# Two transformer layers on one core: the product of weights and values as fp32r over two turned query blocks, issued ahead of the dense units

## The reference

```
def dilated_attention(q, k, v):          # three windows, merged here into one table of biases
    s = q @ k.T * HEAD_DIM ** -0.5 - slope * distance, masked;  p = exp(s - max)
    o = (p @ v) / sum(p)
y_b = dilated_attention(q, k, v) * silu(b_gate)
...
def stick_breaking_mixer(h, k, v, ...):
    z = einsum('bhtd,bhsd->bhts', q, k)                       # per block of 128 queries
    suffix = cumsum(log_keep, axis=3, reverse=True) - log_keep
    weights = where(strict, exp(log_sigmoid(z) + suffix), 0.0)
    o = einsum('bhts,bhsd->bhtd', weights, v)
    return (o * silu(gate)) @ w_out
```

## Time and profile before

| | |
|---|---|
| median of 3 runs | 3656.97 us (3647.4 to 3661.76) |
| profiled execution | 3654.47 us, its span 3652.8 us |
| TensorE busy | 3334.1 us |
| mean granted clock of TensorE | 0.942 of full |
| attention loop, first seven pairs / last | 566 to 1131 us / to 1183 us |
| stick-breaking loop, first seven pairs / last | 2696 to 3346 us / to 3421 us |

### The profile page before, as it was taken

How to read it: one execution, slowest core, us unless ns; L and a number is a source line. 1 busy time by engine, 2 the same in 40 slices (tenths; PEclk the granted TensorE clock), 3 DMA queues, 4 the chain that set the end, 5 groups by cost and what they waited for, 6 DMA issues and landing times. The chain is left out here.

```text
span 3652.8 us, 45164 instructions
## 1 busy us (share of the span) xinstructions
PE 3334.1 (91%) x16644; PEld 2762.9 (76%) x16644; DVE 1664.7 (46%) x2233; ACT 1315.7 (36%) x1783; POOL 539.9 (15%) x430
## 2 busy tenths in 40 slices
PE   6999989999998999698988889888889999998899
PEld 5788878888887777475866767666678888887777
DVE  4343224444444332556556565565434455454333
ACT  4332114444444222323222331223245555555331
POOL 3110000000000001212020020210223333332110
PEclk9999999999999999699999999999889999998799
DMA  2111222211211222012121121211211111111221
GB/s 89 44 52 54 69 69 61 67 60 53 64 52 58 99 78 77 20 48 57 47 58 42 46 64 42 52 47 58 76 35 41 41 41 41 41 41 47 98 69 58
DMA packets 85626, 206.06 MB, mean 56 GB/s; under 512 B 6816, under 2 KB 42272, under 8 KB 85184
## 3 DMA queue, kind: packets, MB, share of 16 engines
q1 hardware_dynamic: 74048, 164.66, 14.6%
q0 software_dynamic: 11392, 38.80, 3.7%
HBM read 165.56 MB, written 21.10 MB: 51 GB/s over the span
## 5 line engine op out<-in xcount | busy, mean ns | idle before, releaser
L119 DVE TENSOR_TENSOR wlo<-wraw,whi 128x1024 fp32r<-128x1024 f32 x208 | 282.0, 1356 | 388.0 <-ACT whi L114 384.7
L114 ACT ACTIVATE whi<-wraw 128x1024 fp32r<-128x1024 f32 x208 | 218.7, 1052 | 525.4 <-PE ssm_pT L127 155.0
L2117 DVE TENSOR_TENSOR_SCAN stick_keep<-stick_keep 128x128 f32<-128x128 f32 (+7 forms) x128 | 188.4, 1472 | 198.4 <-ACT stick_rows L2038 198.2
L125 PE MATMUL ssm_D<-x1hi,whi 128*128 128x512 f32 x640 | 262.1, 410 | 4.5 <-DVEq L1691 4.4
L125 PE MATMUL b_D<-x1hi,whi 128*128 128x512 f32 x640 | 255.3, 399 | 9.9 <-DVE att_k_low L950 8.5
L127 PE MATMUL ssm_D<-x1hi,wlo 128*128 128x512 f32 x640 | 254.5, 398 | 0.0
L126 PE MATMUL ssm_D<-x1lo,whi 128*128 128x512 f32 x640 | 254.3, 397 | 0.0
L127 PE MATMUL b_D<-x1hi,wlo 128*128 128x512 f32 x640 | 251.6, 393 | 0.0
L126 PE MATMUL b_D<-x1lo,whi 128*128 128x512 f32 x640 | 251.4, 393 | 0.0
L125 PE MATMUL stick_D<-x1hi,whi 128*128 128x512 f32 x512 | 221.2, 432 | 6.5 <-DVE x1lo L152 6.5
L2258 POOL TENSOR_TENSOR stick_rows<-stick_rows,stick_keep 128x128 f32<-128x128 f32 (+7 forms) x128 | 161.6, 1263 | 342.4 <-DVE stick_keep L2117 342.4
(11 more groups left out here) (376 smaller groups left out, 7528.8 us busy)
## 6 DMA issues: line engine op xcount, KB each, us to landing
wraw<-w_dram SPq DMA_DIRECT2D x208, 512.0 KB, 3.6
sq<-acum_rows SPq DMA_DIRECT2D x32, 512.0 KB, 9.0
att_bias<-alibi_dram SPq DMA_DIRECT2D x16, 512.0 KB, 3.6
stack<-stack POOLq DMA_DIRECT2D x32, 256.0 KB, 3.3
x_sb<-xT_dram SPq DMA_DIRECT2D x8, 512.0 KB, 8.2
branch_a<-sq POOLq DMA_DIRECT2D x8, 512.0 KB, 3.5
stack<-att_q_low POOLq DMA_DIRECT2D x16, 256.0 KB, 3.5
y_b<-att_y POOLq DMA_DIRECT2D x8, 512.0 KB, 3.0
```

The source lines that it names most:

```text
L114: act.activation(self.whi[:, s, :, :], self.wraw[:, s, :, :], ACT.Copy).then_inc(self.w_hi, 1)
L119: dve.tensor_tensor(self.wlo[:, s, :, :], self.wraw[:, s, :, :], self.whi[:, s, :, :].bitcast(F32), ALU.subtract).then_inc(self.w_lo, 1)
L125: pe.matmul(out, self.whi[:, s, w0, :], xhi[:, k, cols], start=start, stop=False)
L2117: dve.tensor_tensor_scan(k, k, k, 1.0, ALU.mult, ALU.bypass).then_inc(scan, 1)
```

## The change

The product of weights and values is turned round. The values are stationary, as a high and a low part in fp32r, side by side in 128 columns (`v0` for head 0: high, low; `v1` for head 1: low, high), so that the high part's result lies on one half of pO's partitions and the low part's on the other. What moves are the turned weights of two query blocks at a time (a unit u: rows 2u and 2u+1), 256 columns, as high part (`w_high`, a ScalarE copy) and low part (`w_low`, a VectorE subtraction). A group is two key blocks of a unit (up to 512 columns, 384 where the last block belongs to the second row alone). A unit of u % 4 = 0, 1, 2, 3 has 1, 2, 3, 4 groups, 20 in a pair; `turns_of` gives the slots in which they are turned: 2u+2 and 2u+3. Slot 3 and slot 11 get none; slots 2, 4, 5, 7, 10, 12, 13, 15 one; slots 6, 8, 9, 14, 16, 17 two.

In a slot TensorE now takes: scores of row `slot`; `values` of the groups that were turned in slot-1; the dense units; `turn_weights` of this slot's groups. The result needs no turning back. ScalarE takes one half of pO to `part` (`part_y`), VectorE adds the other (`add_y`), in the odd slots from 5 on, and at the pair's end multiplies by the gate once. In attention the rows are normalised on VectorE before they are turned (up to 1024 columns each). `rows` becomes a ring of four rows. v is split when it has been turned (`high_v`, `low_v`), now in slots 17 and 18. The low part of q is written by VectorE straight to the other half of the partitions, with no transfer; attention computes k, q, v, gate in this order (the weights' order in memory follows). The zeroing of k_low moves from VectorE to GpSimd. The stick stage is changed in the same way, without a normalisation; its `low_weights`, `add_y`, `part_y`, `high_v`, `low_v` are the same and lie at the `v_turn` steps 12 and 13.

`norm_diag` goes in all ten norms: `norm_spread` now transposes rtok's columns, each broadcast to 128 columns, in eight transposes.

The diff, cut to its core (attention stage; lines left out as "..."):

```diff
-    def norm_diag(self, dve, diag_done):
-
-        diag = self.sq[:, 0, :].rearrange("p (c t) -> p c t", c=NC)
-        dve.tensor_tensor(diag, self.ident[:, :].unsqueeze(1).to_broadcast([P, NC, P]),
-                          self.rtok[:, :].unsqueeze(2).to_broadcast([P, NC, P]), ALU.mult).then_inc(diag_done, 1)
-
-    def norm_spread(self, pe, spread, diag_done, spread_done):
-        pe.wait_ge(diag_done, 1)
-        for half in range(2):
-            last = pe.matmul(spread[:, half * H:half * H + H], self.ones[:, :],
-                             self.sq[:, 0, half * H:half * H + H], start=True, stop=True)
+    def norm_spread(self, pe, spread, rtok_done, count, spread_done):
+
+        pe.wait_ge(rtok_done, count)
+        for c in range(NC):
+            last = pe.transpose(spread[:, c * P:c * P + P], self.rtok[:, c:c + 1].to_broadcast([P, P]),
+                                self.ident[:, :])
...
-T_GROUPS = [(i + 4) // 4 for _, i in ROWS]
-T_BEFORE = [sum(T_GROUPS[:r]) for r in range(17)]
-T_PAIR = T_BEFORE[16]
+U_GROUPS = [u % 4 + 1 for u in range(8)]
+U_BEFORE = [sum(U_GROUPS[:u]) for u in range(9)]
+G_PAIR = U_BEFORE[8]
+ROW_AT = [(0, 640, 1408, 2304)[r % 4] for r in range(16)]
+ROW_COLS = 3328
+
+
+def turns_of(slot):
+
+    return [(u, g) for u in range(8) for g in range(U_GROUPS[u])
+            if slot == 2 * u + 2 + int(g >= (U_GROUPS[u] + 1) // 2)]
 
...
-    TV, TQ, TK, TG = range(4)
+    TK, TQ, TV, TG = range(4)
...
-        vN, gT, y_sb = (sb(n, [P, 2, S]) for n in ("vN", "gT", "y"))
+        gT, y_sb = sb("gT", [P, 2, S]), sb("y", [P, S])
+        v0 = ctx.enter_context(nc.sbuf_tensor("att_v0", [P, NC, P], F32R))
+        v1 = ctx.enter_context(nc.sbuf_tensor("att_v1", [P, 2, NC, P], F32R))
+        w_high = ctx.enter_context(nc.sbuf_tensor("att_w_high", [P, 2, H], F32R))
+        w_low = ctx.enter_context(nc.sbuf_tensor("att_w_low", [P, 2, H], F32R))
+        part = sb("part", [P, 2 * P])
...
-                        pe.wait_ge(stacked, 64 * p + 64)
+                        pe.wait_ge(q_lo, p + 1)
+                        pe.wait_ge(stacked, 32 * p + 32)
...
-                def turn_weights(p, r):
-                    h, i = ROWS[r]
-                    pe.wait_ge(ex, 16 * p + (r + 1))
-                    for g in range(T_GROUPS[r]):
-                        n = T_BEFORE[r] + g
-                        pe.wait_ge(tcopy, T_PAIR * p + (n + 1))
-                        for b in range(4 * g, min(4 * g + 4, i + 1)):
-                            last = pe.transpose(turned[n % 2][:, (b % 4) * P:(b % 4) * P + P],
-                                                rows[:, r % 2, b * P:b * P + P], K.ident[:, :])
-                        last.then_inc(turn, 1)
-                def values(p, q, r):
-                    h, i = ROWS[r]
-                    if r == 0:
-                        pe.wait_ge(v_copy, 2 * p + 3)
-                    pe.wait_ge(tcopy, T_PAIR * p + (T_BEFORE[r + 1] + 2))
-                    pe.wait_ge(yn, 16 * p + (r + 1))
-                    for b in range(i + 1):
-                        last = pe.matmul(pO[:, 0:HD], wT[:, r % 2, b * P:b * P + P],
-                                         vN[:, q, b * P + HD * h:b * P + HD * h + HD],
-                                         start=b == 0, stop=b == i)
+                def turn_weights(p, u, g):
+                    j, n = u % 4, U_BEFORE[u] + g
+                    pe.wait_ge(even, 16 * p + (2 * u + 2))
+                    pe.wait_ge(t_lo, G_PAIR * p + (n + 1))
+                    col = 0
+                    for b in (2 * g, 2 * g + 1):
+                        for r in (2 * u, 2 * u + 1):
+                            if b <= ROWS[r][1]:
+                                at = ROW_AT[r] + b * P
+                                last = pe.transpose(turned[n % 2][:, col:col + P], rows[:, at:at + P], K.ident[:, :])
+                                col += P
+                    last.then_inc(turn, 1)
+                def values(p, q, u, g):
+                    h, j, n = u // 4, u % 4, U_BEFORE[u] + g
+                    if u == 0:
+                        pe.wait_ge(v_lo, 2 * p + 2)
+                    pe.wait_ge(t_lo, G_PAIR * p + (n + 3))
+                    if g == 0:
+                        pe.wait_ge(y_add, 8 * p + (u + 1))
+                    for b in (2 * g, 2 * g + 1):
+                        v = v1[:, q, b, :] if h else v0[:, b, :]
+                        lone = b == 2 * j + 1
+                        c0 = P if lone else 0
+                        at = 2 * P * (b - 2 * g)
+                        pe.matmul(pO[:, c0:2 * P], v, w_high[:, n % 2, at:at + 2 * P - c0], start=b == 0, stop=False)
+                        last = pe.matmul(pO[:, c0:2 * P], v, w_low[:, n % 2, at:at + 2 * P - c0],
+                                         start=False, stop=lone)
                     last.then_inc(pv, 1)
-                def turn_y(p, g):
-                    if g == 0:
-                        pe.wait_ge(yn, 16 * p + 17)
-                    pe.wait_ge(tcopy, T_PAIR * p + (T_PAIR + 2))
-                    for c in range(4):
-                        last = pe.transpose(turned[g][:, c * P:c * P + P], yN[:, 4 * g + c, :], K.ident[:, :])
-                    last.then_inc(y_turn, 1)
 
                 def pair(p, q, more):
                     u = 0
@@ -748,27 +752,22 @@
                         if slot < 16:
                             score(p, q, slot)
                         n_units = UNITS[slot] if more else int(slot < 2 * KT)
+                        for unit, g in turns_of(slot - 1):
+                            values(p, q, unit, g)
                         units(p + 1, u, u + n_units)
                         u += n_units
-                        if 1 <= slot <= 16:
-                            if slot == 1:
-                                pe.wait_ge(y_out, 2 * p + 2)
-                            turn_weights(p, slot - 1)
-                        if 2 <= slot <= 17:
-                            values(p, q, slot - 2)
-                        if more and slot in (8, 9):
-                            turn_v(p + 1, slot - 8)
-                    for g in range(2):
-                        turn_y(p, g)
+                        for unit, g in turns_of(slot):
+                            turn_weights(p, unit, g)
+                        if more and slot in (17, 18):
+                            turn_v(p + 1, slot - 17)
 
...
+                def high_v(p, q, g):
                     act.wait_ge(v_turn, 2 * p + (g + 1))
                     if not (isinstance(p, int) and p == 0):
-                        act.wait_ge(pv, 16 * p - 14)
-                    act.activation(vN[:, q, g * H:g * H + H], pV[:, :], ACT.Copy).then_inc(v_copy, 1)
+                        act.wait_ge(pv, G_PAIR * p + (U_BEFORE[4] + 2 - G_PAIR))
+                    v = pV[:, :].rearrange("p (c d) -> p c d", d=P)
+                    act.activation(v0[:, 4 * g:4 * g + 4, 0:HD], v[:, :, 0:HD], ACT.Copy)
...
-                def copy_weights(p, r):
-                    h, i = ROWS[r]
-                    act.wait_ge(pv, 16 * p + (r + 1))
-                    for g in range(T_GROUPS[r]):
-                        n = T_BEFORE[r] + g
-                        act.wait_ge(turn, T_PAIR * p + (n + 5))
-                        cols = (min(4 * g + 4, i + 1) - 4 * g) * P
-                        act.activation(wT[:, r % 2, g * H:g * H + cols], turned[n % 2][:, 0:cols],
-                                       ACT.Copy).then_inc(tcopy, 1)
+                def high_weights(p, u, g):
+                    n = U_BEFORE[u] + g
+                    cols = 3 * P if g == u % 4 else 4 * P
+                    act.wait_ge(turn, G_PAIR * p + (n + 5))
+                    act.wait_ge(pv, G_PAIR * p + (n + 1))
+                    act.activation(w_high[:, n % 2, 0:cols], turned[n % 2][:, 0:cols], ACT.Copy).then_inc(t_hi, 1)
+                def part_y(p, u):
+                    h = u // 4
+                    act.wait_ge(pv, G_PAIR * p + (U_BEFORE[u + 1] + 2))
+                    act.wait_ge(y_add, 8 * p + (u + 1))
+                    act.activation(part[HD * h:HD * h + HD, :], pO[HD - HD * h:P - HD * h, 0:2 * P],
+                                   ACT.Copy).then_inc(y_part, 1)
 
                 def pair(p, q, more):
                     for slot in range(19):
                         if slot == 0 and not more:
                             split(p + 1, 1)
+                        for unit, g in turns_of(slot - 1):
+                            high_weights(p, unit, g)
+                        if slot in range(5, 19, 2):
+                            part_y(p, slot // 2 - 2)
                         if slot < 16:
                             weights(p, slot)
                         if slot == 1:
                             gate(p, q)
-                        if 1 <= slot <= 16:
-                            copy_weights(p, slot - 1)
                         if more:
...
```

(59 more changed lines are left out.)

368 lines of the change are left out of this document (188 added, 180 removed).

## The result

| | before | after |
|---|---|---|
| median, us | 3655.05 (3647.4 to 3661.76, 4 runs) | 3954.77 (3952.32 to 3961.89, 4 runs) |
| span of the profiled execution, us | 3652.8 | 3960.4 |
| ratio | 1 | 1.0817, 95% interval 1.0801 to 1.0832 |

What follows compares the result with a forecast made beforehand. TensorE's queue was the bound. Attention +120, stick +136, eighth pairs +12 and +10, norms -12, start -3: +263 on 3654.5 us gives 3917, taken as 3905; range 3790 to 4020.

Steps and rivals of the forecast that it cites:

- The chosen mechanism: In both loops, TensorE waits after the scores for copy and subtraction, plus work queued ahead on ScalarE and VectorE; 60%, 3850 to 3975.
- Rival (a): Both loops: ScalarE's and VectorE's queues are absorbed by longer slots, leaving the short chain only; +165, 3820 us; chance 20%.
- the short chain: Per slot, ScalarE's copy and VectorE's subtraction, less the scores' time: 18.7 us of waits per attention pair, 17.7 in stick.
- (c): Both loops: high and low parts are ready when the scores end, wait per slot under 0.49 us; faster, 3530 with none; 4%.
- (d): Both loops: no change to speak of, waits of 0.5 us per slot; 3650 us; chance 2%.
- Rival (b): TensorE's clock falls in the loops, 7 to 18 us per pair on top; 4000 to 4150 us; chance 14%.
- TensorE's own work: Each pair: 15.1 us of value matmuls become 9.6, yN's transposes and pair-end waits give 1.4; a gain of 6.9 us.
- the waits of both loops: TensorE's idle time before value matmuls, per pair with dense work: 18.7 + 5.4 us in attention, 17.7 + 8.7 in stick.
- the eighth pairs: Last pair of each loop: attention 63 us against 52 from a row's chain on VectorE, +12; stick taken as +10.
- the gain outside the loops: Ten norms -12 us; at the start of attention, first scores need one transfer less, -3 us.
- late queues: ScalarE and VectorE work queued ahead of high or low parts: 5.4 us per attention pair, 8.7 in stick.
- The norms: Ten norms: norm_diag leaves, 1.225 us each; norm_spread's four matmuls become eight transposes of about the same time; -12 us.

## Why the prediction was right, and where its terms were not

It said 3905 us, and 3954.8 was measured, within the range. The chosen mechanism holds: TensorE waits for VectorE's low part between scores and first value product, and the order does it. Rival (a), the short chain alone (3820), is out by 135 us; rivals (c) and (d) are out. Rival (b) is there in its mild form, on top of the forecast instead of in its place. That the sum came out no further off is in part luck: of the +263 us forecast and the +307.6 measured on the profiled executions, TensorE's own work was put 108 us too low, the waits of both loops 45 us and the eighth pairs 11 us too high, and the gain outside the loops 8 us too small. These errors run against each other.

By the windows, per pair with dense work, in us:

| | attention, predicted | measured | stick, predicted | measured |
|---|---|---|---|---|
| TensorE busy | -6.9 | +3.0 | -6.9 | -1.3 |
| TensorE idle | +18.7 + 5.4 = +24.1 | +22.7 | +17.7 + 8.7 = +26.4 | +21.3 |
| pair | +17.2 | +25.7 | +19.5 | +20.0 |

(Measured: busy 576.72 / 7 against 555.64 / 7 and 628.54 / 7 against 637.68 / 7; idle is the rest of each window. The -6.9 held 0.5 us of waits at the pair's end.)

**The waits** were right in attention (24.1 predicted, 22.7 measured) and 5 us too long in stick-breaking, where the 8.7 us of late queues were the weak estimate. In attention they can be compared slot by slot, idle time in front of the value products in us, mean of seven pairs:

| slot | 3 | 5 | 6 | 7 | 8 | 9 | 10 | 11 | 13 | 14 | 15 | 16 | 17 | 18 |
|---|---|---|---|---|---|---|---|---|---|---|---|---|---|---|
| predicted, with late queues | 0.9 | 1.5 | 0.6 | 3.85 | 1.65 | 2.1 | 0.9 | 1.5 | 3.6 | 0.6 | 1.45 | 1.85 | 2.4 | 1.3 |
| measured | 2.6 | 1.5 | 0.4 | 3.2 | 1.0 | 2.0 | 0.7 | 1.5 | 2.9 | 0.3 | 1.4 | 1.2 | 2.35 | 0.65 |

The short chain is right nearly everywhere, the late queues of slots 7, 8, 13 and 16 are each priced 0.6 to 0.7 us too high (for slot 7 the prediction's own figures, 5.55 less 3.4, give 2.15 us and not 2.4), and one late queue was overlooked, that of slot 3. ScalarE computes the gate in slot 1, and its two table loads stand ahead of the exponential of slot 2 and so of slot 3's high part:
```profile
1107.79 1.28 ACT L796 ACT_TABLE_LOAD   x1
1109.09 1.06 ACT L796 ACTIVATE att_gT<-att_gT 128x1024 f32<-128x1024 f32 x1
1110.16 1.28 ACT L812 ACT_TABLE_LOAD   x1
...
1112.07 0.47 ACT L821 ACTIVATE att_w_high<-att_turned 128x384 fp32r<-128x384 f32 x1
```
Scores of this slot were done by 1110.7, the products began at 1113.3. The prediction had counted such loads in stick-breaking only.

**TensorE's own work** is the step that was mis-sized. It was to fall by 6.9 us a pair, and rose by 3.0 in attention and fell by 1.3 in stick-breaking. Two things the runs tell apart.

Where few waits are left (values behind the units, k and q moved, 5.6 us idle a pair, clock 1.00) attention's own work is 522.7 / 7 = 74.7 us, 4.7 less than the 79.4 of before. From one start to the next, without the idle time, the value products took 15.0 us a pair before and take 10.1 there, 0.127 each where I had 0.12. The first product of a slot costs 0.22 us where it had to wait for its low part, and 0.11 where it had not; in that run:
```profile
908.43 0.28 PE L744 MATMUL att_pO<-att_w_high,att_v 128*128 128x256 f32 x1
908.55 0.28 PE L745 MATMUL att_pO<-att_w_low,att_v 128*128 128x256 f32 x1
```
The transposes of yN give 0.8 us. The remaining difference is mostly no work: the dense matmuls just ahead of the products grew by 1.3 us a pair, as the first 0.16 us of a wait lie under the end of the matmul before it and count as busy.

The other 7.7 us of attention come with the waits: 82.4 us a pair at a clock of 0.93. Dense matmuls at 0.42 us behind a wait, as shown above, are the 1.2 GHz level of the clock against 0.23 us at 2.4 GHz. A mean clock of 0.93 over 745 us means some 15 us a pair at the lower level, and if TensorE works in all of it, 15 x (1 - 0.23 / 0.425) = 7 us of it are lost, an estimate. In stick-breaking the same working gives some 4 us more than before (0.92 over 790 us against 0.95 over 650). I had set this case aside since attention's eighth pair kept full clock with idle time in it; with waits in every slot that no longer held, and after the change the eighth pair itself has 0.89. A chance of 14% was too little for it, and as an addition of some 7 us a pair it belonged in the sum. The Trainium skill (TensorE: Matmul & The Clock Gate, The HAM clock gate) says that idle lowers the clock; attention's traces agree, 0.93 with 24 us idle a pair, 0.97 with 7.4, 1.00 with 5.6. Idle time is not all of it: in stick-breaking the clock was 0.95 before, with 1.8 us idle a pair, and no run shows why.

**The eighth pairs**: +12 and +10 predicted; 62 us for 52 is +10, 76 for 75 is +1. Stick's last pair was already set by its chain of scan, GpSimd and copies, which the change leaves.

**The norms**: -12 predicted, -21 measured alone. The step that failed is "four matmuls become eight transposes of about the same time in all". At full clock, in the first norm of before and of after:
```profile
50.53 1.88 PE L216 MATMUL v_turned<-sq,ones 128*128 128x512 f32 x4
```
```profile
49.76 1.04 PE L211 MATMUL v_turned<-ident,rtok 128*128 128x128 f32 x8
```
And in a norm of the dt stage, at half clock:
```profile
1515.27 3.78 PE L216 MATMUL dt_spread<-sq,ones 128*128 128x512 f32 x4
```
```profile
1710.72 1.97 PE L211 MATMUL dt_spread<-ident,rtok 128*128 128x128 f32 x8
```
So each norm saves 0.8 to 1.8 us here, on top of the 1.2 us of the diagonal matrix.

**normalise**: the forms of the operation after (busy us, mean ns):
```profile
L925 DVE TENSOR_SCALAR att_rows<-att_rows,att_rinv 128x1024 f32<-128x1024 f32 x16 | 12.1, 753 | 0.6
...
L925 DVE TENSOR_SCALAR att_rows<-att_rows,att_rinv 128x512 f32<-128x512 f32 x16 | 7.8, 487 | 0.6
```
512 columns more cost 0.27 us, 0.52 ns each, about half of the 1.22 us for 1024 columns of a two-source operation. The rule of the Trainium skill that I had weighed (VectorE: DVE Perf Modes, What auto-detection actually checks) is borne out in its rate, with 0.75 instead of the 0.6 us I had worked out from it. My sum had used at most 1.2.

Added up: 7 x 25.7 + 7 x 20.0 + 10 + 1 - 21 = +310 us; the spans differ by 307.6, and the stretches outside the loops by -23.

## What to carry to other kernels

When products move forward in the queue of the engine that sets the time, write down for every slot which copies on other engines lie between what they read and what they need, and what work covers those copies: here one unit of 0.7 us ahead of the products was worth 130 us in all, and taking all cover away cost 326. A whole slot of lead takes the wait away too, but look then for the next waits in line: here two of them came up, and the version with the lead was 30 us slower than the one with the products behind the dense units. And price an idle bottleneck twice, once for the wait and once for the slower clock behind it.

## What was not expected of the hardware

- With waits of 0.3 to 3.2 us in 14 slots of each pair, the mean granted clock of attention's first seven pairs is 0.93 where it was 1.00. The cost, some 7 us a pair by the estimate above, is near a third of the idle time itself.
- Spreading a norm over the partitions with two fp32 matmuls by a matrix of ones (four instructions of 512 columns) takes 1.88 us at full clock and 3.78 at half, with eight fp32 transposes of 128 columns 1.04 and 1.97 us.
- A true fp32 product of 64 columns takes 0.21 us in the loops; all that the redirected product took off TensorE's own work was 4.7 us of 79.4 in an attention pair, at full clock.
- A 256-column fp32r product that had to wait has its successor 0.22 us behind it, one that had not 0.11 to 0.12.
